# Summing, norming and storing the MoE outputs by lists of tokens, one list for each router group, instead of by token tiles at the end

## What is computed

```
g_idx = argmax(h @ w_rg + b_rg)                      # one of 4 groups per token
e_top, e_idx = top_k(logits of the 4 experts of that group, 2)
gates = softmax(e_top) * p_group
ids = g_idx * 4 + e_idx                              # two of 16 experts, both in one group
out = sum over e of gates[e] * ((silu(h @ w_gate[e]) * (h @ w_up[e])) @ w_down[e])
y = rmsnorm(x + out) * final_norm_g                  # y_prompt 512 rows, y_sample 64 rows
```

## Time and profile before

| | us |
|---|---|
| time, median of 3 | 491.68 (491.62 to 493.36) |
| the profiled execution: its own time | 491.68 |
| its span, first to last instruction | 489.9 |
| TensorE busy | 440.4 (90%) |
| VectorE (DVE), ScalarE (ACT), GpSimd (POOL) busy | 250.1, 156.5, 91.9 |

### The profile page before, as it was taken

How to read it: one execution, slowest core, us unless ns; L and a number is a source line. 1 busy time by engine, 2 the same in 40 slices (tenths; PEclk the granted TensorE clock), 3 DMA queues, 4 the chain that set the end, 5 groups by cost and what they waited for, 6 DMA issues and landing times.

```text
span 489.9 us, 7956 instructions
## 1 busy us (share of the span) xinstructions
PE 440.4 (90%) x3093; PEld 304.1 (62%) x3093; DVE 250.1 (51%) x597; ACT 156.5 (32%) x355; POOL 91.9 (19%) x156
## 2 busy tenths in 40 slices
PE   6999899999999999999999989799999999998200
PEld 5879799887999678778888868333333433433000
DVE  4877715378568436776756468333312112111086
ACT  6664540375244653832413230111011111111021
POOL 4239100201000001010100023201211122122044
PEclk9999999999999999999999995999999999999755
DMA  8905401303000940051011099999999999950394
GB/s 299 224 16 174 172 9 26 146 1 137 36 2 9 255 153 1 22 173 44 0 44 66 1 349 418 343 415 343 397 372 399 424 413 417 416 212 34 122 343 180
DMA packets 31823, 93.18 MB, mean 190 GB/s; under 512 B 8969, under 2 KB 12177, under 8 KB 25649
## 3 DMA queue, kind: packets, MB, share of 16 engines
q1 hardware_dynamic: 27728, 82.81, 46.4%
q0 software_dynamic: 4064, 9.97, 5.3%
HBM read 85.75 MB, written 11.80 MB: 199 GB/s over the span
## 4 chain that ended last, share of the span: by engine, by line
PE 78%; DVE 10%; DMA 6%; ACT 3%; issue 1%; POOL 1%; SPq 0%; POOLq 0%; DVEq 0%; ACTq 0%
PE ps L2085 17%; PE ps L2064 8%; PE ps L1733 8%; PE ps L1735 7%; PE ps L1734 7%; PE ps L1946 3%; PE ps L2039 3%; PE ps L1948 3%; PE ps L1947 3%; DMA pair<-y_pairs 2%; DVE x L1664 2%; PE ps L1971 2%; DMA h_rows<-s_buf 1%; PE ps L1779 1%; ACT s_buf L927 1%
## 5 line engine op out<-in xcount | busy, mean ns | idle before, releaser
L2085 PE MATMUL ps<-we_gu,xT 128*32 128x512 f32 x768 | 84.9, 594 | 0.7 <-ACT xT L1038 0.6
L2085 PEld LDWEIGHTS ps<-we_gu,xT 128*32 128x32 f32 x768 | 24.5, 110 | 52.3 <-issue 50.2
L1733 PE MATMUL ps<-hT_hi,w_hi 128*128 128x288 f32 x160 | 48.5, 303 | 1.6 <-DVE w_lo_q L1108 0.8
L2064 PE MATMUL ps<-we_d,hhT 128*32 128x512 f32 x384 | 43.5, 592 | 1.3 <-DVE hhT L1649 1.3
L1640 DVE TENSOR_TENSOR hh<-sg,ps 128x256 f32<-128x256 f32 x12 | 5.1, 421 | 70.3 <-ACT sg L1054 70.3
L1733 PE MATMUL ps<-w_hi,hT_hi 128*128 128x512 f32 x96 | 38.8, 405 | 0.1
L1734 PE MATMUL ps<-w_lo,hT_hi 128*128 128x512 f32 x96 | 37.5, 390 | 0.0
L1733 PEld LDWEIGHTS ps<-hT_hi,w_hi 128*128 128x128 f32 x160 | 30.1, 188 | 5.0 <-issue 2.5
L1054 ACT ACTIVATE sg<-ps 128x256 f32<-128x256 f32 x12 | 4.6, 384 | 86.6 <-PE ps L2085 86.6
L2064 PEld LDWEIGHTS ps<-we_d,hhT 128*32 128x32 f32 x384 | 13.0, 110 | 29.0 <-issue 29.0
L854 ACT ACTIVATE w_hi<-ring,g_col 128x512 fp32r<-128x512 f32 (+1 forms) x48 | 28.7, 678 | 0.1
(11 more groups left out here) (389 smaller groups left out, 957.7 us busy)
## 6 DMA issues: line engine op xcount, KB each, us to landing
we_gu<-in_w_gate SPq DMA_DIRECT2D x16, 1024.0 KB, 9.2
we_gu<-in_w_up SPq DMA_DIRECT2D x16, 1024.0 KB, 11.0
we_d<-in_w_down SPq DMA_DIRECT2D x16, 1024.0 KB, 10.5
ring<-in_w_in SPq DMA_DIRECT2D x4, 2048.0 KB, 7.9
pair<-y_pairs SPq DMA_DIRECT2D x8, 512.0 KB, 7.6
ring<-in_w_in SPq DMA_DIRECT2D x3, 1024.0 KB, 8.2
x_first<-in_x_p SPq DMA_DIRECT2D x4, 512.0 KB, 9.8
x<-in_x_p SPq DMA_DIRECT2D x4, 512.0 KB, 3.7
```

The lines of the kernel that those rows point to most:

```text
L1733: pe.matmul(out, stationary[0], moving[0], start=c == 0, stop=False)
L2064: last = pe.matmul(ps[cols, 4 + 2 * (b % 2) + half, :], hhT[:, f, cols], we_d[u][:, f, 512 * half:512 * half + 512], start=f == 0, stop=f ...
L2085: last = pe.matmul(ps[cols, 0, :], xT[:, c, cols], we_gu[u][:, :, c, :], start=c == 0, stop=c == KC - 1)
```

## The change

Every token gets a place in a list. Lists 0 to 2 ("early") hold up to 128 tokens of router groups 0, 1 and 2; all others (group 3, what exceeds 128, and tokens of an expert with more than 96 pairs) go on "late" tiles of 128, at least two and at most five. DVE marks the tokens (`mark_late`, `mark_rows`, `tile_table`, some 45 small operations in turn 0), TensorE counts and builds the lists (`count_late`, `rows_of_tiles`). x is stored to DRAM (`x_dram`), so that it can be gathered by list. When a turn's scatters have landed, POOL gathers the list of that group (x and the pairs, 4 and 8 KB a token) while the next turn runs; DVE, ACT and POOL sum, square, norm and scale it in the first and second block of the turn after, and POOL scatters it to y_prompt and y_sample by two indirect DMAs that skip what is not theirs. The third early list and the two late tiles are done after the last turn. `y_dram` is first filled with zeros. ACT, DVE and POOL run turn 1 unrolled too. x is no longer kept in SBUF through the turns.

```diff
+        x_dram = nc.dram_tensor("x2_rows", (TOK, D), F32, kind="Internal").ap()
...
+                if k == RING:
+                    sp.wait_ge(consts, 2)
+                    for part in range(PAIRS // P):
+                        sp.dma_start(y_dram[part * P:(part + 1) * P, :],
+                                     qbd[:, :, :, :].rearrange("p a m k -> p (a m k)")).then_inc(dram_rows, 16)
...
+            def store_x(t):
+                sp.wait_ge(x2_ready, 2 * t + 2)
+                sp.dma_start(x_dram[tok(t), :], x[0:rows_of(t), t, :]).then_inc(dram_rows, 16)
             for t in range(PROMPT_TILES - 1):
                 store_h2(t)
+                store_x(t)
...
             expert(0, 0, 0, 2)
             store_h2(PROMPT_TILES - 1)
+            store_x(PROMPT_TILES - 1)
...
+            store_x(NT - 1)
...
-            pairs = y_dram.rearrange("(t a) d -> t (a d)", a=2)
-            for t in range(NT):
-                for i in range(2):
-                    cols = slice(i * D, (i + 1) * D)
-                    sp.dma_start(pair[0:rows_of(t), t, cols], pairs[tok(t), cols]).then_inc(pair_in[i][t], 16)
-            for t in range(NT):
-                store_out(t)
-            sp.wait_ge(out_stored, 16 * (4 + NT))
+            sp.wait_ge(early_stored, 32 * more + 32 * extra + 32 * TURNS - 32)
+            sp.wait_ge(late_stored, 32 * LEAST_LATE)
+            sp.sem_inc(consts, 1)
...
+            pool.wait_ge(dram_rows, 16 * (PAIRS // P))
...
-            with pool.Fori(1, more + TURNS) as i:
...
+            y_rows = y_dram.rearrange("(t a) d -> t (a d)", a=2)
+            def rows_by(dst, src, tokens, signal):
+                pool.indirect_dma_start(dst, None, src, bass.IndirectOffsetOnAxis(ap=tokens, axis=0),
+                                        bounds_check=TOK - 1, oob_is_err=False).then_inc(signal, 16)
+            def out_by(src, rows, signal):
+                for k, (dst, n) in enumerate(((io["y_p"], SEQ), (io["y_s"], DEC))):
+                    pool.indirect_dma_start(dst, bass.IndirectOffsetOnAxis(ap=rows[:, k:k + 1], axis=0), src, None,
+                                            bounds_check=n - 1, oob_is_err=False).then_inc(signal, 16)
+            def early_gather(n, column):
+                if not (isinstance(n, int) and n == 0):
+                    pool.wait_ge(early_final, n)
+                    pool.sem_inc(dma_cleared, 1)
+                pool.tensor_copy(now_gates[:, :], tile_gates[:, :, bass.ds(column, 1)].rearrange("p a c -> p (a c)")
+                                 ).then_inc(early_idx, 1)
+                pool.tensor_copy(now_rows[:, :], tile_rows[:, bass.ds(column, 1), :].rearrange("p c a -> p (c a)")
+                                 ).then_inc(early_idx, 1)
+                pool.wait_ge(early_idx, 2 * n + 2)
+                pool.sem_inc(dma_cleared, 1)
+                rows_by(early_x[:, :], x_dram, now_rows[:, 0:1], early_in)
+                rows_by(early_pair[:, :], y_rows, now_rows[:, 0:1], early_in)
+            def early_norm(n):
+                pool.wait_ge(early_ssq, n + 1)
...
+            def early_store(n, column):
+                pool.wait_ge(early_final, n + 1)
...
+                out_by(early_out[:, :], now_out, early_stored)
+            def group_stored(i):
                 for b in range(PER):
-                    gather_next(i, b)
-                    scatter_later(i, b)
+                    pool.wait_ge(stored[b], 16 * i + 16)
+                pool.sem_inc(dma_cleared, 1)
+            gather_next(1, 0)
+            scatter_later(1, 0)
+            gather_next(1, 1)
+            scatter_later(1, 1)
+            pool.wait_ge(dram_rows, 16 * (PAIRS // P) + 16 * NT)
+            pool.wait_ge(rows_ready, 1)
+            group_stored(1)
+            early_gather(0, 0)
+            gather_next(1, 2)
+            scatter_later(1, 2)
+            for k in range(LEAST_LATE):
+                rows_by(late_x[k][:, :], x_dram, tile_rows[:, EARLY_TILES + k, 0:1], late_x_in[k])
+            with pool.Fori(2, more + TURNS) as i:
+                gather_next(i, 0)
+                scatter_later(i, 0)
+                early_norm(i - 2)
+                gather_next(i, 1)
+                scatter_later(i, 1)
+                early_store(i - 2, i - 2)
+                group_stored(i)
+                early_gather(i - 1, i - 1)
+                gather_next(i, 2)
+                scatter_later(i, 2)
+                pool.wait_ge(early_stored, 32 * i - 32)
+                pool.sem_inc(dma_cleared, 1)
...
+            last_early = more + TURNS - 2
+            group_stored(more + TURNS)
+            for k in range(LEAST_LATE):
+                rows_by(late_pair[k][:, :], y_rows, tile_rows[:, EARLY_TILES + k, 0:1], late_in[k])
+            early_norm(last_early)
+            early_store(last_early, last_early)
+            for k in range(LEAST_LATE):
+                pool.wait_ge(late_ssq, k + 1)
...
+                pool.tensor_tensor(tile_stats[:, 2, 1 + k:2 + k], tile_stats[:, 1, 1 + k:2 + k], neghalf[:, 0:1],
+                                   ALU.pow).then_inc(late_rstd, 1)
+            for k in range(LEAST_LATE):
+                pool.wait_ge(late_final, k + 1)
+                out_by(late_pair[k][:, D:2 * D], tile_rows[:, EARLY_TILES + k, :], late_stored)
...
+                    if b == 0 and not isinstance(i, int):
+                        early_squares(i - 2)
+            def early_squares(n):
+                act.wait_ge(early_sum, 2 * n + 2)
+                act.activation(early_pair[:, 0:D], early_x[:, :], ACT.Square,
+                               accum_out=tile_stats[:, 0, 0:1]).then_inc(early_ssq, 1)
...
+                    if i is first and b == 0:
+                        mark_late()
+                    if i is first and b == 1:
+                        mark_rows()
+                    if b == 0 and not isinstance(i, int):
+                        early_sums(i - 2)
+                    if b == 1 and not isinstance(i, int):
+                        early_scale(i - 2)
+            def early_sums(n):
+                dve.wait_ge(early_in, 32 * n + 32)
+                for k in range(2):
+                    dve.scalar_tensor_tensor(early_x[:, :], early_pair[:, k * D:(k + 1) * D], now_gates[:, k:k + 1],
+                                             early_x[:, :], ALU.mult, ALU.add).then_inc(early_sum, 1)
+                    dve.wait_ge(early_sum, 2 * n + k + 1)
+            def early_scale(n):
+                dve.wait_ge(early_rstd, n + 1)
+                dve.scalar_tensor_tensor(early_out[:, :], early_x[:, :], tile_stats[:, 2, 0:1], gf_bc[:, :],
+                                         ALU.mult, ALU.mult).then_inc(early_final, 1)
...
+            early_sums(more + TURNS - 2)
+            early_scale(more + TURNS - 2)
+            for k in range(LEAST_LATE):
+                column = EARLY_TILES + k
+                dve.wait_ge(late_x_in[k], 16)
+                dve.wait_ge(late_in[k], 16)
                 for i in range(2):
-                    dve.wait_ge(pair_in[i][t], 16)
-                    dve.scalar_tensor_tensor(x[0:r, t, :], pair[0:r, t, i * D:(i + 1) * D], gates[0:r, i, t:t + 1],
-                                             x[0:r, t, :], ALU.mult, ALU.add).then_inc(sum_ready, 1)
-                    dve.wait_ge(sum_ready, 2 * t + i + 1)
...
-            dve.wait_ge(gates_ready, 1)
...
+                    dve.scalar_tensor_tensor(late_x[k][:, :], late_pair[k][:, i * D:(i + 1) * D],
+                                             tile_gates[:, i, column:column + 1], late_x[k][:, :], ALU.mult,
+                                             ALU.add).then_inc(late_sum, 1)
+                    dve.wait_ge(late_sum, 2 * k + i + 1)
+            for k in range(LEAST_LATE):
+                dve.wait_ge(late_rstd, k + 1)
+                dve.scalar_tensor_tensor(late_pair[k][:, D:2 * D], late_x[k][:, :], tile_stats[:, 2, 1 + k:2 + k], gf_bc[:, :],
+                                         ALU.mult, ALU.mult).then_inc(late_final, 1)
...
+            def count_late():
+                pe.wait_ge(marks_late, 1)
+                pe.matmul(ps[:, 3, 384:385 + NT], earlier[:, :], of_row[:, 3, 0:NT + 1], start=True, stop=False)
+                pe.matmul(ps[:, 3, 384:385 + NT], ones[:, :], of_row[:, 4, 0:NT + 1], start=False,
+                          stop=True).then_inc(late_counted, 1)
+            def rows_of_tiles():
+                pe.wait_ge(marks_rows, 1)
+                for t in range(NT):
+                    r = rows_of(t)
+                    last = pe.matmul(ps[:, 3, 392:392 + 24], row_hot[0:r, t, :],
+                                     row_vals[0:r, t, :, :].rearrange("p v c -> p (v c)"), start=t == 0, stop=t == NT - 1)
+                last.then_inc(rows_made, 1)
...
+                    if i is first and b == 1:
+                        count_late()
                     if i is first and b == PER - 1:
+                        rows_of_tiles()
```

(44 more changed lines are left out.)

138 lines of the change are left out of this document (117 added, 21 removed).

## The result

The changed kernel takes 519.04 us (median of 4, 518.36 to 519.45) where the kernel before takes 492.52 (median of 4): a ratio of 1.0515, 95% interval 1.0491 to 1.0540. It is slower by 26.5 us, where 2.5 were forecast and the range ended at 499.5. The span grew from 489.9 to 515.7, by 25.8.

What follows compares the result with a forecast made beforehand. TensorE was taken to set the pace, with no room in the weight stream beside it, then a serial tail. 489.9 - 7.3 + 1.3 + 1.5 + 7.0 = 492.4, that is +2.5 on 491.7: 494.2 us, range 488 to 499.5.

Steps and rivals of the forecast that it cites:

- no extra tile runs: Late tiles after the last turn: two hold 256 tokens, 212 are late, so no shortening of the tail was excluded.
- A: Serial tail after the last scatter's landing: shrinks from 28.4 to 21.1 us, 7.3 us less.
- B: Start of the expert stage: the fourth store of x pushes back the last store of h, 1.3 us more.
- C: TensorE in the first group: seven small f32 matmuls counting and building lists, 1.5 us more.
- D: Gathers inside the weight stream: 4.21 MB of extra list bytes cost TensorE 7.0 us.
- rival 3: Clock: more TensorE idling before the first block and in groups 2 and 3 costs 2.5 us, 496.7; chance 0.12.
- two readings: What TensorE loses in the weight stream: 5.7 us if weights wait, 8.3 if lists wait; the middle, 7.0, taken.
- The eighth of the stream: POOL's queue in the weight stream: a gather of h rows moved at some 52 GB/s, so weights are favoured.
- the third that was worked out from it: Queues alternating by packet: 4 KB rows against 8 KB weight pieces get a third, lists in time, loss 5.7 us.
- (1): Weight stream: the lists ride along without holding TensorE, loss 0 to 2 us, time 487.2 to 489.2; chance 0.20.
- (2): POOL becomes the chain: slow list stores delay gathers of h rows in the last two groups, 499 us; chance 0.18.
- Costed at nothing: Zero writes to y_pairs, list building on DVE, early sums and POOL's added waits: all hidden in idle time, 0 us.

Runs made afterwards that it cites:

- e1: The changed kernel with a branch ahead of the loop over extra late tiles, entered only if their number is above zero; 503.83 us, ratio 1.0209.
- e2: e1 with the fourth store of x moved behind the weights of expert 3; 504.37 us, ratio 1.0216.
- e5: e4 with both last stores of x moved behind the first four down weights; 500.42 us, ratio 1.0131.
- e4: e1 with the five list-building matmuls between the third block's gate/up and down matmuls, apart from the overflow slots' matmuls; 502.09 us, ratio 1.0171.
- e3: e1 with the three early lists holding no rows, all instructions kept, their tokens' outputs left out; 497.58 us, ratio 1.0080.
- e7: e5 with the late tiles' gathers of x after the last turn and the three early lists empty; 494.18 us, ratio 1.0013.
- e8: The kernel before, unchanged, run once more with a profile on another chip; 493.42 us (one run).

## Why the prediction was wrong

**The step that failed** is the sentence that no extra tile runs because two late tiles hold 256 tokens and 212 are late. The count was right; the inference from it was not. A loop of length zero ran its body once on three engines, and 14.8 of the 25.8 us are that. The program's order has the untested jump, and the tested one on SP beside it; I read the order for what stands ahead of what, and not for how a loop is entered. Without the empty tile the time (503.83 in e1) would still lie beyond the forecast's range: the tail (A) gained 4.3 us less than its term, and the clock, which the sum put at nothing, cost 6.0.

The other terms, from e1's trace where the empty tile is gone, else from the changed kernel's:

| term | forecast | measured |
|---|---|---|
| A, the tail | -7.3 | -3.0 (28.4 to 25.4) |
| B, start of the stage | +1.3 | +1.9 |
| C, list building on TensorE | +1.5 | +1.7 |
| D, lists in the weight stream | +7.0, all waits | +4.1 of waits |
| clock in blocks 0, 3 and 9 | 0 (rival 3: +2.5) | +1.6, +1.7, +2.7 |
| y of the last block | 0 | +0.3 |
| empty tile | excluded | +14.8 |

They sum to 25.8. B differs from run to run: in e1's trace the first transposes start 3.4 later than before, not 1.9.

**A** was mis-sized by 4.3. The first late gather is issued 0.96 after the last scatter's landing, as forecast (0.9). e1's rows from there:

```profile
478.14 1.03 POOL L842 DMA_INDIRECT late_pair<-y_pairs,tile_rows  x1 [3.19 <-DMA y_pairs<-y,now_pair]
479.47 1.02 POOL L842 DMA_INDIRECT late_pair<-y_pairs,tile_rows  x1 [0.30 <-issue]
...
487.03 2.60 DVE L1905 SCALAR_TENSOR_TENSOR late_x<-late_pair,tile_gates,late_x 128x1024 f32<-128x1024 f32 x2 [0.43 <-DMA late_pair<-y_pairs,tile_rows]
...
492.31 2.06 POOL L848 DMA_INDIRECT out_y_p<-late_pair,tile_rows  x1 [0.19 <-issue]
...
497.20 0.96 POOL L848 DMA_INDIRECT out_y_s<-late_pair,tile_rows  x1 [0.30 <-issue]
```

The second gather lands 9.7 after the scatter (477.18 to 486.9), not 7.2, and the last output goes out 20.0 after it, not 17.9: 2.1 us. The gathers were mis-sized: their bytes were priced at the 411 GB/s of the full stream, and the DMA moved 239 GB/s from 479.5 to 482.0, 331 to 484.5 and 162 to 487.0; from the second gather's landing to the last issue 10.3 us passed, 10.7 were allowed. The last output lands at 499.8, a little sooner than allowed (2.6 instead of 3.2). The forecast ended there, but the span goes on for 2.8 us; before, the last store landed at 489.5, only 0.4 ahead of the end. That is the rest, and what fills it no row shows: no DMA moves in it.

**B** had the right mechanism: the store of h lands 10.1 after its issue in e1 and 8.0 in e2, which lacks that store of x ahead of it. That no hole in the DMA takes these bytes nearer the gather, e2 shows; behind the down weights (e5) they are out of its way.

**C** was right in size. Its place cost as much again in clock (e4), which no term held.

**D**: the total of block 9's neighbourhood, 6.8 with the clock, is near the 7.0, but not for the reason given. The forecast took the middle of two readings and leaned to the second, that the lists are late and DVE waits for them. DVE's rows behind hhT in turns 2 and 3:

```profile
399.67 0.41 DVE L1862 COPY hhT<-ps 128x256 f32<-128x256 f32 x1
400.00 2.60 DVE L1876 SCALAR_TENSOR_TENSOR early_x<-early_pair,now_gates,early_x 128x1024 f32<-128x1024 f32 x2
...
441.76 0.42 DVE L1862 COPY hhT<-ps 128x256 f32<-128x256 f32 x1
442.09 2.60 DVE L1876 SCALAR_TENSOR_TENSOR early_x<-early_pair,now_gates,early_x 128x1024 f32<-128x1024 f32 x2
```

No wait: the lists were there, and TensorE waited for weights (3.53). The eighth of the stream that I gave POOL's queue came from one gather with at most a scatter beside it, and pauses between; from 357 to 434 us before, that queue had 15.4% of the engines' time. With several in flight its share is larger (376 to 392, then 420 to 432; packets, MB, share of 16 engines' time):

```profile
q0 software_dynamic: 491, 1.85, 29.4%
...
q0 software_dynamic: 458, 1.33, 27.9%
```

The rule of the Trainium skill (DMA: Bandwidth & Descriptors, Queues, rings and completion order), that an engine takes turns between its queues packet by packet, was weighed and set aside for the earlier trace rows. These shares are nearer to the third that was worked out from it than to the eighth; that the engines took turns they don't show, since from 376 to 392 us 491 packets of POOL's queue stand beside 642 of the other. The reading that it favoured, weights wait and lists are in time, was the right one: 4.1 us of waits, where that reading gave 5.7.

**Rivals.** (1) did not happen: e3 gains 6.3 us without bytes, and the stream moved 412 GB/s from 363 to 423 us, hardly more than before (411). (2) did not: the waits of POOL are in e3 and e7 too, and no block behind the first waits for xg. (3) did: three falls of the clock cost 6.0 us, more than twice what it was priced at; one of them, in block 3, needed no idle time, and one is partly there in the kernel before. **Costed at nothing** and found so: the zeros of y_pairs (TensorE is busy 59.54 of 60 us from 60 to 120, 59.28 before) and DVE's list building (blocks 1 to 3 grow by the small matmuls and the clock).

No version that was run beats the kernel before. e7, which leaves the lists' work out, equals it, so moving the lists within this scheme could win about what the start and the late gathers lose there, 2.9 us by an estimate from e7's 1.5 and 1.4.

## What to carry to other kernels

Ask of every loop with a length from memory whether its body can be skipped at all, and read that from the program's order, not from the source; a count that should be zero deserves a test ahead of the loop. Work that is put "beside" a stage bound by TensorE may still displace bytes that TensorE needs: price it against the slack of the transfers behind it in time, and add what the clock loses after the wait. A queue's share measured with one or two transfers in flight says little of its share with several.

## What the hardware showed

- A loop whose length is read as zero ran once (14.8 us here); a branch ahead of it removes that.
- The granted clock fell to 0.50 (1.2 GHz) behind 2.8 us of small f32 matmuls in a row (347.22 to 350.02) with no idle time, and 8.77 instead of 7.07 us followed; with the first of them elsewhere it stayed at 2.4 GHz (e4).
- Behind idle times of 1.9 to 5.4 us before block 0 the first gate and up matmuls took between 7.07 and 8.84 us, not in the order of the idle times: 7.07 after 2.82 (before), 7.60 after 2.54 (e8), 8.62 after 1.86 (e5). Idle time alone does not tell what the clock does there; the activity ahead of it differed too, and what decides stays open.
- After the last output's landing 2.8 us pass to the end of the span where POOL's indirect DMA makes it (e1, e7), and 0.4 where SP's does (before). Not explained.
